# Retention's output projections of two heads by seven half-size products

## The chip, the core and the metric

One core of a Trainium2 chip runs two transformer blocks of two layers each over 512 tokens of width 1024. The metric is device microseconds of one execution; lower is better. All inputs and weights lie in the chip's main memory as 32-bit floats.

## The reference, cut to what matters

The change lies in the retention layer of the second block: four heads, each with 256 query and key features and 512 value features.

```
proj = h @ w_in                              # q, k: 4 x 256; v, g: 4 x 512 columns
q, k = rotate(q), rotate(k) * dk ** -0.5
...                                          # y = decayed attention of each head: scores, decay, values
mu, var = mean(y), var(y)                    # per head
y = ((y - mu) * rsqrt(var + EPS)).reshape(B, S, H * dv)
return (silu(g) * y) @ w_out                 # w_out: 2048 x 1024
```

The last line is what is changed. For head h it is a product of 512 tokens by 512 features (silu(g)*y of that head) with rows 512h to 512h+511 of `w_out`; the four heads' products are added to the residual.

## The kernel before

**Numbers.** Every 32-bit operand is split into two values of a reduced format, hi = round(x) and lo = x - hi, and each product is made of three matmuls, hi·hi, hi·lo and lo·hi. A matmul takes a 128x128 stationary operand and 512 moving columns.

**The weight units.** Weights come in units of up to 128x2048, numbered in one list made by `plan()`; even units use slot 0 and odd units slot 1 of `w_raw`, `w_hi` and `w_lo`. A unit goes through four queues, each of which takes the units in the order of the list:

- SyncE (SP) issues the load into `w_raw` when the unit two places earlier has its low part (semaphore `w_lo_ready`), since then its raw slot is free.
- ScalarE (ACT), in `act_split`, copies `w_raw` to `w_hi` when the load has landed and TensorE has finished the unit two places earlier (`blocks_done`).
- GpSimd (POOL) makes `w_lo = w_raw - w_hi` in four quarters of 512 columns (`split_low`, L749), each of which counts up `w_lo_ready`.
- TensorE (PE) waits in `pe_weights` until the unit's quarters are there.

**Retention.** The head loop is written out as five steps. Step n projects head n and, before and between that, attends with head n-1: scores, query projection `q` (one unit), values, key projection `k`, transposition of the gated values, value projection (units `v0`, `v1`), gate projection (`g0`, `g1`). Steps 1 and 2 end with `output()` for heads 0 and 1: units `o0` and `o1` are the left and right 512 columns of the head's `w_out` rows, each 512 features deep. `output()` runs over 2 halves, 4 token tiles and 4 feature chunks with 3 matmuls each, so 96 matmuls per head (L853 to L855), into PSUM banks 4 to 7; VectorE (DVE) adds each finished bank to the residual (L2528). Heads 2 and 3 are projected in the later steps, which the change leaves as they are.

**Around the place.** The gate projection leaves its four tiles in banks 0, 1, 6 and 7, and ACT takes each through Silu (L2376, semaphore `ret_g_in`). `output()` begins in banks 4 and 5, and waits for `ret_g_in` only ahead of its tiles in banks 6 and 7. After `output()` TensorE makes the next step's scores (L1781, banks 2 to 4) and then the `q` unit (L842 to L844, banks 0 and 1). DVE multiplies the scores by the decay (L3140), ACT copies the result to its hi part (L2342), DVE makes its lo part (L3143); the values' matmuls (L1795) need them.

Of the kernel before, what the change touches and what calls it, by code (L numbers as in the profile page):

```python
# [138 lines left out]
RET_LAST_BANKS = (6, 7, 4, 5, 0, 1, 2, 3)  # L139
RA_PARTS = ((0, 512), (512, 512), (1024, 256))  # L140
# [99 lines left out]
def plan():  # L240
# [70 lines left out]
    for h in range(RH + 1):  # L311
        if h < RH:
            for x in "qk":
                unit(f"ret.{x}{h}"), done(f"ret.{x}{h}", 0, 1)
            for x in "vg":
                for part in range(2):
                    unit(f"ret.{x}{part}{h}"), done(f"ret.{x}{part}{h}", *range(TT))
        if h:
            for half in range(2):
                unit(f"ret.o{half}{h - 1}")  # L320
                if h < RH:
# [15 lines left out]
for _n, (_name, _dmas) in enumerate(UNITS):  # L337
# [21 lines left out]
           for kind, stages, events in SHARED for n, stage in enumerate(stages) for event, total in events.items()}  # L359

# [30 lines left out]
def memory(nc, ctx, dram):  # L391
# [52 lines left out]
    m.ry, m.rg, m.ra = view(2048, 2048, TT), view(4096, 2048, TT), view(6144, 1280)  # L444
    m.rv_hi, m.rv_lo = (r[:, :].rearrange("p (t d) -> p t d", t=TT) for r in (m.r_hi, m.r_lo))
# [292 lines left out]
def pool_program(m, pool):  # L738
# [80 lines left out]
    plain(last_down(f"sw0.d{G2 - 1}"), INDEX["sw1.d0"])  # L819
# [909 lines left out]
def pe_retention(m, pe, beside):  # L1729
# [4 lines left out]
    def step(i, hs, project, attend, write=True):  # L1734
# [8 lines left out]
        def features(x, j):  # L1743
            names = [f"ret.{x}{n}" for n in hs]
            if j == 0:
                pe_weights(m, pe, names, i)
            if x == "k" and not first:
                left("q_in", 2, j + 1)
            elif not first:
                left_before("g_in", TT, TT)  # L1750
            bank = b[2 + j] if first and x == "k" else b[j]
            pe_features(m, bank[:, :], weight(m, names, 2048, KC), j * P, h, KC)

        def tokens(x, part):
# [3 lines left out]
            for t in range(TT):  # L1758
# [4 lines left out]
                elif part == 0 and hs[0] > 1:  # L1763
                    pe.wait_ge(*m.upto("ret_acc", along(i, [KC * (n - 2) + KC for n in hs])))
# [8 lines left out]
        def scores():  # L1773

            left_before("k_roped", 1, 1)
            for kb in (0, 1, 3, 2):
                bank, at = TURN_AT[kb]
                if kb == 2 and project and hs[0] > 1:
                    pe.wait_ge(*m.upto("ret_acc", along(i, [KC * (n - 2) + 5 for n in hs])))
# [5 lines left out]
        def values():  # L1785
# [3 lines left out]
            for q in range(TT):  # L1789
                if q == 3 and project and hs[0] > 1:  # L1790
                    pe.wait_ge(*m.upto("ret_acc", along(i, [KC * (n - 2) + 6 for n in hs])))
# [27 lines left out]

        def held(half, tiles):  # L1820
# [4 lines left out]
            for n in tiles:  # L1825
                if half:
                    pe.wait_ge(*m.upto("ret_acc", KC * h + n + 1))
# [5 lines left out]
        def last_output():  # L1833
            h = RH - 1
            for n, (half, tile) in enumerate(RET_TAIL):
# [3 lines left out]
                if n < 2:  # L1839
                    pe.wait_ge(*m.upto("ret_acc", KC * (h - 1) + 7 + n))  # L1840
# [43 lines left out]
def pe_program(m, pe):  # L1884
# [24 lines left out]
    pe_input(m, pe, "sw1", "sw1_normed", normed, "ret_acc", KC * RH, "sw1.g0", True)  # L1909
# [419 lines left out]
def act_retention(m, act):  # L2329
    s, b, run = m.sem, m.bank, m.nc.scalar.activation  # L2330

    def step(i, hs, project, attend, write=True):
# [27 lines left out]
        if attend:  # L2360
            for c in range(4):
# [3 lines left out]
                run(m.act_hi[:, c if project else RET_SLOTS[c], :], b[2 + c][:, :], ACT.Copy).then_inc(s("ret_o_hi"), 1)  # L2365
        if project:
            for x in "vg":
                for part in range(2):
                    names = [f"ret.{x}{part}{n}" for n in hs]
                    if (x, part) != ("v", 0):  # L2370
                        split(after(names))
                if x == "g" and attend:
# [39 lines left out]
def act_program(m, act):  # L2412
# [21 lines left out]
    act_rms(m, act, "sw1", "ret_acc", [KC * (RH - 1) + n for n in RET_COMPLETE], "sw1.g0", "sw1.u0")  # L2434
# [666 lines left out]
def dve_retention(m, dve, end):  # L3101
    s, b, v = m.sem, m.bank, m.nc.vector

    def step(i, hs, project, attend, write=True):
# [40 lines left out]
        def held(n):  # L3145
            h = RH - 2
            dve_add_block(m, dve, "ret", n, b[RET_BANKS[n % 4]], [f"ret.o{n // 4}{h}"], n % 4, None, [h], False)

        def low(c, at):
            left_before("o_hi", 4, c + 1)  # L3150
            v.tensor_tensor(m.act_lo[:, at, :], b[2 + c][:, :], m.act_hi[:, at, :].bitcast(F32), ALU.subtract).then_inc(s("ret_o_lo"), 1)
# [5 lines left out]
        else:  # L3157
            held(0), held(1)
# [20 lines left out]
        if project:  # L3179
            take("k")  # L3180
            if attend:
                for c in range(4):
                    low(c, c)
# [4 lines left out]
            if attend and write:  # L3188
                for n in range(KC):
                    dve_add_block(m, dve, "ret", n, b[4 + n % 4], [f"ret.o{n // 4}{h - 1}" for h in hs], n % 4, i, [h - 1 for h in hs], hs[0] == 1)  # L3190
# [9 lines left out]
        def add(n):  # L3200
            half, tile = RET_TAIL[n]
            block = TT * half + tile
            dve_add_block(m, dve, "ret", block, b[RET_LAST_BANKS[n]], [f"ret.o{half}{RH - 1}"], tile, None, None, False, False, KC * (RH - 2) + block + 1)
# [138 lines left out]
```

## Time and profile before

| | before |
|---|---|
| device time, median of 3 runs | 2459.97 us (2458.8 to 2460.01) |
| span of the profiled execution, first to last instruction | 2456.9 us |
| what lies around the span (median minus span) | 3.07 us |
| TensorE busy | 2442.6 us, 99% of the span |
| DVE, ACT, POOL busy | 61%, 40%, 50% |
| mean granted TensorE clock | 0.999 of full speed |

The profiled execution shows a span and no device time of its own beside it; the last 3.07 us of the median are taken as what lies around every span. Busy times of TensorE count overlapping matmuls once; the pace of the matmuls is read from the distance of their starts.

### The profile page before, as it was taken

Reading aid. Unit: us, or ns where it says so; the run is one execution under the profiler, and the core shown is the slowest. Engines: PE = TensorE matmul, PEld = TensorE weight load, DVE = VectorE, ACT = ScalarE, POOL = GpSimd, SP = SyncE. Lnnn points to the kernel's source line nnn. Section 1 sums busy time; section 2 is a strip of 40 time slices with the busy share of each in tenths; the row PEclk is TensorE's granted clock in tenths of the full one; section 3 lists DMA queues with packets and bytes.
Section 4 is the critical chain, followed back from the end, with each engine's and each line's share of the span. In section 5 each row is a group of like instructions: output and inputs, shape, how many; then the busy total and the mean of one; then the engine's idle time right before and its main releaser. Section 6 shows DMA issues by size and latency. Waiting matters only on the chain.

```text
span 2456.9 us, 32036 instructions
## 1 busy us (share of the span) xinstructions
PE 2442.6 (99%) x11945; PEld 2032.3 (83%) x11945; DVE 1490.0 (61%) x1999; ACT 988.5 (40%) x1352; POOL 1232.8 (50%) x879
## 2 busy tenths in 40 slices
PE   9999999999999999999999999999999999999998
PEld 8778888888888888888888888888888888888887
DVE  6657777786585777784334566666224133466667
ACT  4445444444565444444324333333332223433332
POOL 4224555644333555553323566665444443566664
PEclk9999999999999999999999999999999999999999
DMA  5212333332222233333221322333222322233222
GB/s 182 68 52 91 103 102 102 103 120 87 70 69 86 86 103 102 102 103 104 69 69 60 126 96 96 102 103 122 93 86 69 103 69 86 95 103 101 96 97 83
DMA packets 173704, 230.94 MB, mean 94 GB/s; under 512 B 11670, under 2 KB 128540, under 8 KB 173468
## 3 DMA queue, kind: packets, MB, share of 16 engines
q1 hardware_dynamic: 173596, 229.44, 28.5%
q8 instruction: 75, 1.23, 0.2%
q14 instruction: 33, 0.27, 0.0%
HBM read 227.32 MB, written 2.10 MB: 93 GB/s over the span
## 4 chain that ended last, share of the span: by engine, by line
PE 65%; issue 20%; POOL 11%; DVE 2%; ACT 0%; DMA 0%; POOLq 0%; SPq 0%; DVEq 0%; ACTq 0%
PE banks L842 11%; PE banks L843 11%; PE banks L844 11%; POOL w_lo L749 11%; PE banks L1640 6%; PE banks L1639 6%; PE banks L1641 6%; PE banks L853 1%; PE banks L855 1%; PE banks L854 1%; PE banks L1125 1%; PE banks L1146 1%; PE banks L1094 1%; PE banks L1081 1%; PE banks L1100 1%
## 5 line engine op out<-in xcount | busy, mean ns | idle before, releaser
L749 POOL TENSOR_TENSOR w_lo<-w_raw,w_hi 128x512 fp32r<-128x512 f32 (+1 forms) x820 | 1163.9, 1451 | 1204.8 <-ACT w_hi L1921 1187.6
L1921 ACT ACTIVATE w_hi<-w_raw 128x2048 fp32r<-128x2048 f32 x204 | 390.4, 1914 | 457.5 <-PE banks L844 176.7
L842 PE MATMUL banks<-h_hi,w_hi 128*128 128x512 f32 x1448 | 567.3, 392 | 0.3 <-POOL w_lo L749 0.3
L844 PE MATMUL banks<-h_hi,w_lo 128*128 128x512 f32 x1448 | 563.5, 389 | 0.0
L843 PE MATMUL banks<-h_lo,w_hi 128*128 128x512 f32 x1448 | 563.4, 389 | 0.0
L842 PEld LDWEIGHTS banks<-h_hi,w_hi 128*128 128x128 f32 x1448 | 271.8, 188 | 62.0 <-issue 4.2
L843 PEld LDWEIGHTS banks<-h_lo,w_hi 128*128 128x128 f32 x1448 | 271.9, 188 | 56.9 <-issue 1.2
L844 PEld LDWEIGHTS banks<-h_hi,w_lo 128*128 128x128 f32 x1448 | 271.8, 188 | 56.8
L2528 DVE TENSOR_TENSOR x_residual<-x_residual,banks 128x512 f32<-128x512 f32 x103 | 69.9, 685 | 132.1 <-PE banks L855 85.7
L3026 DVE TENSOR_TENSOR work<-banks,work 128x512 f32<-128x512 f32 x44 | 30.4, 691 | 191.7 <-PE banks L844 191.7
L1639 PE MATMUL banks<-w_hi,act_hi 128*128 128x512 f32 x352 | 136.9, 389 | 0.0
L1640 PE MATMUL banks<-w_lo,act_hi 128*128 128x512 f32 x352 | 136.9, 389 | 0.0
L1641 PE MATMUL banks<-w_hi,act_lo 128*128 128x512 f32 x352 | 136.9, 389 | 0.0
L3068 DVE TENSOR_TENSOR work<-work,banks 128x1024 f32<-128x1024 f32 x80 | 97.7, 1221 | 18.7 <-PE banks L1641 9.9
L2225 ACT ACTIVATE act_hi<-work 128x1280 fp32r<-128x1280 f32 x26 | 33.2, 1276 | 184.1 <-DVE work L2935 184.1
L1639 PE MATMUL banks<-split_hi,act_hi 128*128 128x512 f32 x264 | 102.7, 389 | 0.0
L1640 PE MATMUL banks<-split_lo,act_hi 128*128 128x512 f32 x264 | 102.7, 389 | 0.0
L1641 PE MATMUL banks<-split_hi,act_lo 128*128 128x512 f32 x264 | 102.7, 389 | 0.0
L2629 DVE CUSTOM_DVE_ANT_0 work<-banks,consts 128x128 f32<-128x128 f32 (+3 forms) x128 | 57.4, 488 | 70.9 <-PE banks L1136 25.7
L1768 PE MATMUL banks<-w_hi,h_hi 128*128 128x512 f32 x256 | 99.9, 390 | 0.0
L1770 PE MATMUL banks<-w_hi,h_lo 128*128 128x512 f32 x256 | 99.6, 389 | 0.0
L1769 PE MATMUL banks<-w_lo,h_hi 128*128 128x512 f32 x256 | 99.6, 389 | 0.0
(330 smaller groups left out, 4672.1 us busy)
## 6 DMA issues: line engine op xcount, KB each, us to landing
w_raw<-in_ffn_w_in SPq DMA_DIRECT2D x44, 1024.0 KB, 5.1
w_raw<-in_ffn_w_up SPq DMA_DIRECT2D x32, 1024.0 KB, 5.3
w_raw<-in_ffn_w_down SPq DMA_DIRECT2D x52, 512.0 KB, 4.4
w_raw<-in_ret_w_in SPq DMA_DIRECT2D x24, 1024.0 KB, 5.1
w_raw<-in_ffn_w_out SPq DMA_DIRECT2D x36, 512.0 KB, 4.4
w_raw<-in_diff_w_qkv SPq DMA_DIRECT2D x12, 1024.0 KB, 5.1
w_raw<-in_fox_w_in SPq DMA_DIRECT2D x12, 1024.0 KB, 5.3
w_raw<-in_ret_w_out SPq DMA_DIRECT2D x8, 1024.0 KB, 5.0
```

The lines of the kernel that those rows point to most:

```text
L749: nc.gpsimd.tensor_tensor(m.w_lo[:, sl, at], m.w_raw[:, sl, at], m.w_hi[:, sl, at].bitcast(F32), ALU.subtract)\
L842: mm(out, hi, x[0][:, k, :], start=k == 0, stop=False)
L843: mm(out, hi, x[1][:, k, :], start=False, stop=False)
L844: last = mm(out, lo, x[0][:, k, :], start=False, stop=k == kc - 1)
L1639: mm(out, hi, w[0], start=begin, stop=False)
L1640: mm(out, hi, w[1], start=False, stop=False)
L1641: last = mm(out, lo, w[0], start=False, stop=end)
L1768: mm(out, hi, w[0][:, k, :], start=part == 0 and k == 0, stop=False)
L1769: mm(out, hi, w[1][:, k, :], start=False, stop=False)
L1770: last = mm(out, lo, w[0][:, k, :], start=False, stop=part == 1 and k == 3)
L1921: m.nc.scalar.activation(m.w_hi[:, sl, 0:width], m.w_raw[:, sl, 0:width], ACT.Copy).then_inc(m.sem("w_hi_ready"), 1)
L3068: v.tensor_tensor(out, out, bank, ALU.add).then_inc(s(f"{t}_evicted"), 1)
```

## The change

For heads 0 and 1 the product is split in halves in tokens, features and columns. With X11, X12, X21, X22 the quarters of the head's features (first index: tokens 0 to 255 or 256 to 511; second: features) and W11 to W22 those of its weights, seven products of half size take the place of eight:

| product | left factor | right factor | unit, part | banks |
|---|---|---|---|---|
| P1 | X11 | W11 | o0, 0 | 2, 3 |
| P2 | X12 | W21 | o0, 1 | 4, 5 |
| P5 | S1 = X21 + X22 | T1 = W12 - W11 | o1, 0 | 6, 7 |
| P3 | S4 = X12 - S2 | W22 | o1, 1 | 0, 1 |
| P6 | S2 = S1 - X11 | T2 = T3 + W11 | c, 0 | 2, 3 |
| P4 | X22 | T4 = W21 - T2 | c, 1 | 4, 5 |
| P7 | S3 = X11 - X21 | T3 = W22 - W12 | d, 0 | 6, 7 |

Each product is 2 token tiles of 2 feature chunks with 3 matmuls: 12 matmuls, 84 per head. Two units per head are new, `c` (128x2048, made by DVE in the raw slot of `o0`) and `d` (128x1024, T3 in a token buffer); they have no load. DVE makes S1 to S4 and T1 to T4, and adds the products in 11 operations instead of 8.

```diff
@@ plan()
+            if h <= RET_PRODUCED:
+                unit(f"ret.c{h - 1}", 0), unit(f"ret.d{h - 1}", 0)
+                for x, part in OUT_ORDER:
+                    done(f"ret.{x}{h - 1}", part)
@@ pool_program
+        for part in range(QUARTERS):
+            at = slice(256 * part, 256 * part + 256)
+            nc.gpsimd.tensor_tensor(m.w_lo[:, d % 2, at], m.out_t3[:, at], m.w_hi[:, d % 2, at].bitcast(F32), ALU.subtract)\
+                .then_inc(s("w_lo_ready"), 1)
@@ pe_retention, scores()
+            if project and hs[0] > 1:
+                pe.wait_ge(*m.upto("ret_added", NADDS * (hs[0] - 2) + out_added(OUT_P4)))
@@ pe_retention, output()
             left_before("o_lo", 4, 4)
-            for half in range(2):
-                names = [f"ret.o{half}{n - 1}" for n in hs]
-                pe_weights(m, pe, names, i)
-                for n in range(4):
-                    if half:
-                        left_before("acc", KC, n + 1)
-                    elif n >= 2:
-                        left("g_in", TT, n + 1)
-                    pe_tokens(m, b[4 + n][:, :], weight(m, names, 2048, 4), (m.act_hi[:, 0:4, :], m.act_lo[:, 0:4, :]), 4, n, 512)\
-                        .then_inc(s("blocks_done"), 1)
+            left_before("o_summed", 5, 5)
+            left("g_in", TT, TT)
+            for product in OUT_ORDER:
+                unit, part = product
+                name, bank, x = f"ret.{unit}{head}", OUT_BANKS[product], x_of[product]
+                pe_weights(m, pe, [name], None, QUARTERS if part or unit == "d" else 2)
...
+                held_by = {OUT_P6: OUT_P1, OUT_P4: OUT_P2, OUT_P7: OUT_P5}.get(product)
+                if held_by:
+                    pe.wait_ge(*m.upto("ret_added", NADDS * head + out_added(held_by)))
+                for t in range(2):
+                    last = pe_tokens(m, b[bank + t][:, :], w, x, 2, t, 512)
+                last.then_inc(s("blocks_done"), 1)
@@ act_retention
-            split(after([f"ret.o0{n - 1}" for n in hs]))
+            head = hs[0] - 1
             if write:
-                split(after([f"ret.o1{n - 1}" for n in hs]))
+                act.wait_ge(*m.upto("ret_o_mixed", 4 * head + 2))
+            split([f"ret.o1{head}"])
+            if write:
+                act.wait_ge(*m.upto("ret_o_mixed", 4 * head + 4))
+                split([f"ret.c{head}"])
+                act.wait_ge(*m.upto("blocks_done", BLOCK[f"ret.o1{head}", 0]))
+                run(m.w_hi[:, slot([f"ret.d{head}"]), 0:1024], m.out_t3, ACT.Copy).then_inc(s("w_hi_ready"), 1)
+                split(after([f"ret.d{head}"]))
@@ dve_retention
+            if project and hs[0] > 1:
+                dve.wait_ge(*m.upto("ret_added", NADDS * (hs[0] - 1)))
...
             if attend and write:
-                for n in range(KC):
-                    dve_add_block(m, dve, "ret", n, b[4 + n % 4], ...
+                feature_sums(), feature_sums_low()
+                out_weight_sums(hs[0] - 1)
+                add_products(hs[0] - 1)
```

On TensorE, at the start of step 1's `output()` (the last matmul of `g1`, then the first of `o0`; `w_hi`, `act_hi` are the stationary and moving parts), the rows of before are:

```order
L1770 MATMUL banks<-w_hi,h_lo 128x512
L853 MATMUL banks<-w_hi,act_hi 128x512 [waits w_lo_ready,ret_o_lo]
L854 MATMUL banks<-w_lo,act_hi 128x512
L855 MATMUL banks<-w_hi,act_lo 128x512
L853 MATMUL banks<-w_hi,act_hi 128x512
```

and of the changed kernel:

```order
L1809 MATMUL banks<-w_hi,h_lo 128x512
L890 MATMUL banks<-w_hi,act_hi 128x512 [waits ret_g_in,w_lo_ready,relu_mlp_mixed,ret_o_lo]
L891 MATMUL banks<-w_lo,act_hi 128x512
L892 MATMUL banks<-w_hi,act_lo 128x512
L890 MATMUL banks<-w_hi,act_hi 128x512
```

The wait for `ret_g_in` (all four Silu tiles) has moved from the 25th matmul of the stage to its first. `relu_mlp_mixed` is a semaphore that the sums S1 to S4 share with an earlier stage.

On ACT, from the last Silu of step 1 to the first operation of step 2 (`work<-banks` is Silu, each `w_hi<-w_raw` a unit's high part), before, where the three units are `o1`, the next step's `q` and its `k`:

```order
L2376 ACTIVATE work<-banks 128x512 [waits blocks_done] x3
L1921 ACTIVATE w_hi<-w_raw 128x2048 [waits blocks_done,w_landed1]
L1921 ACTIVATE w_hi<-w_raw 128x2048 [waits blocks_done,w_landed0]
L1921 ACTIVATE w_hi<-w_raw 128x2048 [waits blocks_done,w_landed1]
L2342 ACTIVATE act_hi<-work 128x512 [waits ret_decayed] x2
```

and of the changed kernel, where they are `o1`, `c`, `d`, `q` and `k`:

```order
L2433 ACTIVATE work<-banks 128x512 [waits blocks_done] x3
L1972 ACTIVATE w_hi<-w_raw 128x2048 [waits blocks_done,w_landed1,relu_mlp_w_mixed]
L1972 ACTIVATE w_hi<-w_raw 128x2048 [waits blocks_done,w_landed0,relu_mlp_w_mixed]
L2444 ACTIVATE w_hi<-tokbuf 128x1024 [waits blocks_done]
L1972 ACTIVATE w_hi<-w_raw 128x2048 [waits blocks_done,w_landed0]
L1972 ACTIVATE w_hi<-w_raw 128x2048 [waits blocks_done,w_landed1]
L2393 ACTIVATE act_hi<-work 128x512 [waits ret_decayed] x2
```

`q` now stands behind `c` and `d`. Its slot (slot 0) was that of `o0` and is now that of `c`, so its load, its high part and its low part each wait for `c` where they waited for `o0`.

## Rows read from the trace of the kernel before

**Rows 1.** The page: span, and busy time of TensorE.

```profile
span 2456.9 us, 32036 instructions
PE 2442.6 (99%) x11945; PEld 2032.3 (83%) x11945; DVE 1490.0 (61%) x1999; ACT 988.5 (40%) x1352; POOL 1232.8 (50%) x879
```

**Rows 2.** The page: the chain that ended last, by engine.

```profile
PE 65%; issue 20%; POOL 11%; DVE 2%; ACT 0%; DMA 0%; POOLq 0%; SPq 0%; DVEq 0%; ACTq 0%
```

**Rows 3.** TensorE's waits, the longest in total: us, times, longest one.

```profile
PE banks L878 <- DVE x_residual L2575: 2.6, 6, 1.0
```

**Rows 4.** Busy time by stretch: step 1's output, step 2's scores, step 2's output.

```profile
core 0: us, PE busy (x) PEld busy (x) DVE busy (x) ACT busy (x) POOL busy (x), PEclk, DMA share, GB/s
...
1841.36:1863.12 21.76, 21.76 (x98) 18.02 (x96) 4.82 (x7) 4.32 (x3) 10.07 (x8) 1.00 0.30 97
1863.12:1867.24 4.12, 4.12 (x17) 2.55 (x16) 1.85 (x3) 2.54 (x2) 1.88 (x2) 1.00 0.25 97
1941.30:1963.10 21.80, 21.80 (x97) 18.05 (x97) 4.81 (x7) 4.32 (x3) 10.07 (x8) 1.00 0.31 97
```

**Rows 5.** TensorE in order of time: start, us; gate's last matmul, output's first.

```profile
1841.13 0.39 PE L1770 MATMUL banks<-w_hi,h_lo 128*128 128x512 f32 x1
1841.36 0.39 PE L853 MATMUL banks<-w_hi,act_hi 128*128 128x512 f32 x1
```

**Rows 6.** ACT in order of time: the last Silu, then units o1 and q.

```profile
1841.56 0.60 ACT L2376 ACTIVATE work<-banks 128x512 f32<-128x512 f32 x1 [2.12 <-PE banks L1770]
1842.05 1.91 ACT L1921 ACTIVATE w_hi<-w_raw 128x2048 fp32r<-128x2048 f32 x1
1852.50 1.92 ACT L1921 ACTIVATE w_hi<-w_raw 128x2048 fp32r<-128x2048 f32 x1 [8.54 <-PE banks L855]
```

**Rows 7.** A wait's end on TensorE elsewhere: the releasing DVE operation, then the matmul.

```profile
202.95 1.29 DVE L2575 SCALAR_TENSOR_TENSOR x_residual<-work,x_columns,tokbuf 128x1024 f32<-128x1024 f32 x1
...
204.38 0.30 PE L878 MATMUL banks<-consts,x_residual 128*128 128x128 f32 x1 [1.03 <-DVE x_residual L2575]
```

**Rows 8.** POOL in order of time: four quarters each.

```profile
1464.34 7.03 POOL L749 TENSOR_TENSOR w_lo<-w_raw,w_hi 128x512 fp32r<-128x512 f32 x4 [3.07 <-ACT w_hi L1921]
...
1765.82 5.92 POOL L749 TENSOR_TENSOR w_lo<-w_raw,w_hi 128x512 fp32r<-128x512 f32 x4 [6.28 <-ACT w_hi L1921]
...
1854.49 5.03 POOL L749 TENSOR_TENSOR w_lo<-w_raw,w_hi 128x512 fp32r<-128x512 f32 x4 [5.41 <-ACT w_hi L1921]
1865.36 5.46 POOL L749 TENSOR_TENSOR w_lo<-w_raw,w_hi 128x512 fp32r<-128x512 f32 x4 [5.85 <-ACT w_hi L1921]
```

**Rows 9.** SP: the issue of one load (v0 of step 2).

```profile
1859.69 0.37 SPq L521 DMA_DIRECT2D w_raw<-in_ret_w_in  x1
```

**Rows 10.** Loads, median us from issue to landing: 1800 to 1950 us, then 1837 to 1848 us.

```profile
w_raw<-in_ret_w_in SPq DMA_DIRECT2D x9, 1024.0 KB, 5.2
w_raw<-in_ret_w_out SPq DMA_DIRECT2D x4, 1024.0 KB, 5.0
...
w_raw<-in_ret_w_in SPq DMA_DIRECT2D x1, 1024.0 KB, 6.3
```

**Rows 11.** DVE in order of time around step 1's output.

```profile
1820.43 0.69 DVE L3186 TENSOR_TENSOR split_lo<-banks,split_hi 128x512 fp32r<-128x512 f32 x1 [2.03 <-ACT split_hi L2376]
1844.28 0.69 DVE L2528 TENSOR_TENSOR x_residual<-x_residual,banks 128x512 f32<-128x512 f32 x1 [23.16 <-PE banks L855]
...
1865.03 0.69 DVE L3140 TENSOR_TENSOR work<-banks,tokbuf 128x512 f32<-128x512 f32 x1 [1.03 <-PE banks L1781]
...
1867.97 3.74 DVE L3143 TENSOR_TENSOR act_lo<-work,act_hi 128x512 fp32r<-128x512 f32 x3
```

**Rows 12.** Groups of DVE by shape: count, busy us, mean ns, idle before.

```profile
L3068 DVE TENSOR_TENSOR work<-work,banks 128x1024 f32<-128x1024 f32 x80 | 97.7, 1221 | 18.7 <-PE banks L1641 9.9
...
L2907 DVE TENSOR_TENSOR tokbuf<-w_raw 128x1024 f32<-128x1024 f32 x44 | 73.2, 1663 | 0.0
...
L3077 DVE TENSOR_TENSOR x_residual<-x_residual,work 128x1024 f32<-128x1024 f32 x20 | 38.5, 1978 | 0.0
```

More of the change, by code:

```diff
@@ L2371, in step @@
                         split(after(names))
+                    if (x, part) == ("g", 0) and attend and write:
+                        left_before("o_summed", 5, 5)
+                        run(m.act_hi[:, 4:7, :], m.ry[:, 0:3, :], ACT.Copy).then_inc(s("ret_o_sums_hi"), 1)
+                        run(m.act_hi[:, 0:2, 256:512], m.ry[:, 3, :].rearrange("p (k t) -> p k t", k=2), ACT.Copy)\
+                            .then_inc(s("ret_o_sums_hi"), 1)
                 if x == "g" and attend:
@@ new lines, in feature_sums @@
+        def feature_sums():
+            done = s("ret_o_summed")
+            a11, a21, a12, a22 = (m.banks[:, c:c + 2, at:at + 256] for c, at in ((2, 0), (2, 256), (4, 0), (4, 256)))
+            s1, s2, s3, s4 = (m.ry[:, n, :].rearrange("p (k t) -> p k t", k=2) for n in range(4))
+            left_before("turned", 4, 4)
+            v.tensor_copy(s4, a21).then_inc(done, 1)
+            left_before("o_summed", 5, 1)
+            v.tensor_tensor(s1, s4, a22, ALU.add).then_inc(done, 1)
+            v.tensor_tensor(s3, a11, s4, ALU.subtract).then_inc(done, 1)
+            left_before("o_summed", 5, 2)
+            v.tensor_tensor(s2, s1, a11, ALU.subtract).then_inc(done, 1)
+            left_before("o_summed", 5, 4)
+            v.tensor_tensor(s4, a12, s2, ALU.subtract).then_inc(done, 1)
@@ new lines, in feature_sums_low, with out_weight_sums @@
+        def feature_sums_low():
+            left_before("o_sums_hi", 2, 1)
+            v.tensor_tensor(m.act_lo[:, 4:7, :], m.ry[:, 0:3, :], m.act_hi[:, 4:7, :].bitcast(F32), ALU.subtract).then_inc(s("ret_o_sums_lo"), 1)
+            left_before("o_sums_hi", 2, 2)
+            v.tensor_tensor(m.act_lo[:, 0:2, 256:512], m.ry[:, 3, :].rearrange("p (k t) -> p k t", k=2),
+                            m.act_hi[:, 0:2, 256:512].bitcast(F32), ALU.subtract).then_inc(s("ret_o_sums_lo"), 1)
+        def out_weight_sums(head):
+            names, done = [f"ret.o{half}{head}" for half in range(2)], s("ret_o_mixed")
+            for name in names:
+                dve.wait_ge(*m.upto(f"w_landed{slot([name])}", LANDED[INDEX[name]]))
+            (b11, b21), (b12, b22) = [[m.w_raw[:, slot([name]), at:at + 1024] for at in (0, 1024)] for name in names]
+            dve.wait_ge(*m.upto("ret_k_roped", head + 2))
+            v.tensor_tensor(m.out_t3, b22, b12, ALU.subtract).then_inc(done, 1)
+            left_before("o_mixed", 4, 1)
+            v.tensor_tensor(b12, b12, b11, ALU.subtract).then_inc(done, 1)
+            left_before("o_mixed", 4, 2)
+            dve.wait_ge(*m.upto("w_lo_ready", QUARTERS * (INDEX[names[0]] + 1)))
+            v.tensor_tensor(b11, m.out_t3, b11, ALU.add).then_inc(done, 1)
+            left_before("o_mixed", 4, 3)
+            v.tensor_tensor(b21, b21, b11, ALU.subtract).then_inc(done, 1)
@@ new lines, in add_products @@
+        def add_products(head):
+            kept = m.out_p1
+            if head:
+                dve.wait_ge(*m.upto("ret_added", NADDS * head))
+            for n, (source, into) in enumerate(OUT_ADDS):
+                if source == "kept":
+                    more = kept
+                else:
+                    unit, part = source
+                    dve.wait_ge(*m.upto("blocks_done", BLOCK[f"ret.{unit}{head}", part]))
+                    more = m.banks[:, OUT_BANKS[source]:OUT_BANKS[source] + 2, :]
+                earlier = [k + 1 for k in range(n) if out_touched(k) & out_touched(n) - {source if source != "kept" else None}]
+                if earlier:
+                    dve.wait_ge(*m.upto("ret_added", NADDS * head + max(earlier)))
+                if into == "last rows":
+                    x, more = m.x[:, 2:4, :].rearrange("p t (a n) -> p t a n", a=2), kept.unsqueeze(2).broadcast_to([P, 2, 2, 512])
+                else:
+                    x = kept if into == "kept" else quadrant(m, into)
+                if n:
+                    v.tensor_tensor(x, x, more, ALU.add).then_inc(s("ret_added"), 1)
+                else:
+                    v.tensor_copy(x, more).then_inc(s("ret_added"), 1)
@@ L3157, in step @@
         else:
+            dve.wait_ge(*m.upto("ret_added", NADDS * RET_PRODUCED))
             held(0), held(1)
@@ L3182, in step @@
                 for c in range(4):
-                    low(c, c)
+                    low(c, c, 256 if write and c < 2 else T)
             for tile in range(TT):
```

65 lines of the change are left out of this document (48 added, 17 removed).

## Prediction

> **What bounds the kernel now.** The page comes first: TensorE is busy for 2442.6 of 2456.9 us [rows 1], so 14.3 us of the whole span are its idle time. The chain that ended last runs 65% over TensorE and 11% over GpSimd's low parts [rows 2]; the latter are weights that came just in time. The list of TensorE's waits says whether they hold it up: the largest sum is 2.6 us over six waits, the longest one is 1.0 us, and no line of retention stands there [rows 3]. So a matmul that goes shortens the kernel by its pace, and a new wait of TensorE lengthens it by nearly all of its length.
>
> Then the stage itself, by stretches [rows 4]. Step 1's 96 output matmuls take 21.76 us, TensorE busy throughout, at granted clock 1.00 (2.4 GHz): 0.2267 us each. Step 2's differ by 0.04 us, so one head is worked out and doubled. The scores behind them take 4.12 us. DVE is busy for 4.82, ACT for 4.32, POOL for 10.07 of the 21.76 us, so there is room for added work; what matters is its order and its latency.
>
> **What is removed.** 12 matmuls per head, 12 x 0.2267 = 2.72 us, 5.44 us for both. That is 0.22% of the time, and about 0.2% is what a measurement of this kernel can tell from no change; the whole gain would barely show.
>
> **A wait that is moved.** All four Silu tiles must now be out before the first matmul. The last gate matmul starts at 1841.13 and the first of the output followed at 1841.36 [rows 5]. The last Silu starts at 1841.56 and takes 0.60 [rows 6], so it ends at 1842.16. A matmul that waited for DVE started 0.14 us behind the end of its releaser (202.95 + 1.29 = 204.24, then 204.38) [rows 7]. So the first product starts at 1842.30, 0.94 us later than before. All of TensorE's queue stands behind it, and nothing covers it. Bounds: 0.80 without the restart, 0.94 with it.
>
> **The path of the weights.** From 1842.30 a product takes 2.72 us: P1 and P2 end at 1847.74, P5 at 1850.46, P3 at 1853.18, P6 at 1855.90, P4 at 1858.62, P7 at 1861.34; the scores end at 1865.46. Then TensorE wants the next step's `q`. Before, its chain began when `o0` was done: ACT made its high part at 1852.50 [rows 6], POOL was through at 1854.49 + 5.03 = 1859.52 [rows 8], 7.7 us ahead of the use at 1867.24. Now it begins with `c`, in the same slot:
>
> - ACT may split `c` when P2 is done. The o0 unit's last matmul starts at 1841.36 + 47 x 0.2267 = 1852.01 and ACT started at 1852.50, so 0.49 after that start, 0.26 after the pace's end: 1848.00.
> - POOL starts 1.99 us after ACT (1852.50 to 1854.49) and takes 5.03: `c` is ready at 1855.02. P6 wants two quarters, there at 1852.51, at 1853.18, and P4 all of them at 1855.90, so both are covered, by 0.7 and 0.9 us.
> - SP may load `q` only then, 0.17 us later (1859.52 to 1859.69 [rows 9]), at 1855.19. The load takes 5.2 us [rows 10]: 1860.39. P4, which must also be done, ends earlier.
> - ACT, then POOL after 1.99 us: 1860.44 to 1862.43. POOL's pass next to the decays took 5.46 [rows 8], so `q` is ready at 1867.89, and TensorE goes on at about 1867.95.
>
> TensorE stands from 1865.46 to 1867.95: **a new wait of 2.5 us**. Bounds: with a load of 5.0 us [rows 10] and 5.03 for POOL it is 1.8; with 6.3 us for the load, seen once for this very `q`, and 5.92 for both of POOL's passes [rows 8], it is 4.9. I take the middle rows, since they are of the same operations in the same place.
>
> Behind `q` on SP stands the load of `k`, which waits for `d`; it and its two splits follow `q` by some 5.5 us, so `k` is ready near 1873.4 and is wanted 48 x 0.2267 = 10.9 us after `q` starts, at 1878.8. No wait there.
>
> **POOL's neighbour.** The pass at 1854.49 ran while DVE added output tiles, each with one input in PSUM, and took 5.03; that at 1765.82, during DVE's low parts with both inputs in SBUF, took 5.92 [rows 8]. While `c` is in POOL, DVE adds products out of PSUM, so I take 5.03 for it.
> The Trainium skill (GPSIMD Engine Reference, Specifications) states the rule: the SBUF interface is shared, and a DVE instruction with two SBUF inputs contends. The trace agrees, with those 5.03 and 5.92. By the rule the pass over `q` could reach 5.92 as well, since the last add has both inputs in SBUF; the sum below would then be 0.9 us larger over both heads.
>
> **Covered edits.** S1 to S4, their splits and T1 to T4 fall into the gate projection, where DVE was idle for 23.16 us up to 1844.28 [rows 11]. From 1821.1: five 512-wide operations at 0.69, low parts of about 2.5 together, then four 1024-wide at up to 1.66 [rows 12]; T1 to T4 start when `o1` has landed, at about 1832.6, T2 waits for POOL's pass over `o0`, and T4 is done near 1841, 7 us before ACT wants `c`. `o1` splits behind the last Silu as before (1842.05 [rows 6]); its first two quarters are there at 1846.6, P5 wants them at 1847.74. Without these covers each us would be a us of TensorE. `d`'s four 256-wide quarters have no row: between half of a 512-wide quarter (2.5 us for four) and a full one (5.0), in POOL from 1855.02. At worst P7 is late by 1.5 us, and the wait for `q`, which doesn't depend on P7, shortens by as much: nothing either way. I take the lower, nearer by size.
>
> The adds are nine at 1.22, one of 1024 from SBUF (up to 1.98) and one of twice that [rows 12]. Banks are freed in time: the P4 add that the scores wait for ends at about 1860.3, they start at 1861.34. The last adds end near 1866; behind them on DVE stand the decays, which began at 1865.03, and ACT's copies. The low parts they lead to ended at 1867.97 + 3.74 = 1871.7 [rows 11]; 2 us later is still ahead of the values' matmuls at 1878.8.
>
> **The sum.** Per head -2.72 + 0.94 + 2.49 = +0.71 us, +1.4 us for both, on a span of 2456.9: 2458.3. With the 3.07 us that lie around the span the median is 2461.4 us. By the bounds a head comes to between -0.1 and +3.1.
>
> **Rivals.**
> - *Only the Silu wait is new.* `q` would have to be ready 2.5 us sooner than the rows say, sooner even than the lower bound by 1.8. For it: each link was read with other neighbours. Then 2 x (-2.72 + 0.94) = -3.6: 2456.4 us. Chance 0.08.
> - *Neither wait*: -5.4, 2454.5 us. The order of semaphores speaks against it, since the Silu tile can't be out before its matmuls end. Chance 0.04.
> - *Slower: POOL held up by DVE on the way to `q`.* The worst pass in the rows took 7.03 us [rows 8], next to two-input sums. If both the `c` and the `q` pass took that, it would be 2.0 and 1.6 us more per head, +8.6 in all: 2468.6 us. It decides from 1.75 us per head on, where the total passes +4.9. Against: DVE's adds at `c` read PSUM. Chance 0.13.
> - *Slower: the clock falls in the new waits.* TensorE now stands twice in 24 us, once for 2.5 us. If one `q` unit's 48 matmuls then ran at 1.2 GHz, each head would pay 48 x 0.2267 = 10.9 us: 2483 us. Eight matmuls per head at that level (1.8 us) already decide. Against: the granted clock is 1.00 in every stretch [rows 4]. But the longest wait so far is 1.0 us [rows 3]. Chance 0.04. The Trainium skill (TensorE: Matmul & The Clock Gate, Part 1) says that idleness brings the lower level; no stretch here shows it.
>
> **The numbers.** My forecast, two new waits that eat the gain, has 0.71, and its own range by its bounds is 2459.8 to 2466.2. The range reaches down to the first rival and leaves out the most extreme end above, where every link would be at its worst: 2456.4 to 2465.4. Faster by over 0.2% (below 2455.0): the second rival and a little, 0.05. Slower (above 2464.9): the last two and the forecast's upper tail, 0.18. Within: 0.77.
>
> **What the profile after would show.** TensorE waiting for ACT's Silu tile ahead of the first product, 0.9 us, twice. Ahead of L879, the first matmul of `q`, a wait for POOL of 2 to 3 us, twice. 84 matmuls per output at the old pace, with no wait of over 0.3 us between products. SP issuing `q` some 17 us later against the stage's start than before. DVE idle up to the sums, with T4 done before the first product. The prediction is wrong if TensorE waits inside the products (then `c` or `d` is late, or a bank), if it waits at the values (the adds delay the decays), or if the clock in that stretch is below 1.00.

## The result, and the profile after

| | before | after |
|---|---|---|
| device time, median of 4 runs each | 2459.39 us (2458.2 to 2460.01) | 2470.89 us (2468.18 to 2472.17) |
| ratio, 95% interval | | 1.0045 [1.0033, 1.0057] |
| span of the profiled execution | 2456.9 us | 2466.4 us |
| mean granted TensorE clock | 0.999 | 0.998 |

The changed kernel is slower by 0.45%, 9.5 us above the forecast and above its range. Of these 9.5 us, 8.1 lie in the span (2466.4 where 2458.3 was worked out). The other 1.4 are the distance from span to median. Each of the four executions of after took 1.8 us more than its own span, and the profiled one, at 2468.18, was the shortest of them; the longest had a mean clock of 0.996. The medians lie 11.5 us apart and the profiled spans 9.5; what follows explains those 9.5, and no trace shows the other executions of after.

The page of after, its span and busy times:

```profile
span 2466.4 us, 32058 instructions
...
PE 2441.4 (99%) x11921; PEld 2030.1 (82%) x11921; DVE 1535.1 (62%) x2027; ACT 997.3 (40%) x1360; POOL 1259.2 (51%) x895
```

TensorE has lost its 24 matmuls, yet its busy time fell by only 1.2 us against [rows 1], not by 5.4: some of the matmuls that are left ran more slowly. And 25.0 us of the span are idle now, where 14.3 were. Its waits in the two stages (1835 to 1990 us), total, times, longest:

```profile
PE banks L879 <- POOL w_lo L776: 9.3, 2, 5.0
PE banks L890 <- ACT work L2433: 1.8, 2, 0.9
```

There are two waits per head and no others, at the two places that were forecast: the first product behind Silu (0.9 us) and `q` behind POOL. The second is twice as long as forecast, and TensorE runs more slowly behind it. Windows of after (columns as in [rows 4]): the products of both heads, then the wait of head 0 and what follows it.

```profile
1842.35:1861.40 19.05, 19.05 (x84) 15.81 (x85) 11.09 (x9) 5.21 (x4) 12.90 (x12) 1.00 0.26 85
1946.55:1965.60 19.05, 19.02 (x84) 15.80 (x85) 11.09 (x9) 4.56 (x3) 12.90 (x12) 1.00 0.25 84
1865.90:1870.20 4.30, 0.06 (x1) 0.00 (x0) 4.27 (x7) 1.57 (x3) 4.30 (x4) 0.94 0.00 0
1870.20:1872.90 2.70, 2.70 (x6) 2.16 (x7) 1.92 (x2) 0.00 (x0) 2.70 (x2) 0.50 0.52 116
```

The 84 matmuls take 19.05 us where 96 took 21.76 [rows 4]. After the wait the granted clock is 0.50, the level of 1.2 GHz, and six matmuls fill the 2.70 us in which twelve have room. In head 1 eight start at that pace. TensorE in order of time, the first matmuls of `q` in head 0, then the first of head 1:

```profile
1870.20 0.80 PE L879 MATMUL banks<-h_hi,w_hi 128*128 128x512 f32 x1 [4.25 <-POOL w_lo L776]
1870.80 0.63 PE L880 MATMUL banks<-h_lo,w_hi 128*128 128x512 f32 x1
1871.22 0.63 PE L881 MATMUL banks<-h_hi,w_lo 128*128 128x512 f32 x1
...
1975.23 0.62 PE L879 MATMUL banks<-h_hi,w_hi 128*128 128x512 f32 x1 [5.04 <-POOL w_lo L776]
```

Why `q` was late is read off POOL and DVE. POOL's quarters of `q`, the first two of head 0 and the first of head 1:

```profile
1862.71 1.27 POOL L776 TENSOR_TENSOR w_lo<-w_raw,w_hi 128x512 fp32r<-128x512 f32 x1 [4.71 <-ACT w_hi L1972]
1863.94 3.32 POOL L776 TENSOR_TENSOR w_lo<-w_raw,w_hi 128x512 fp32r<-128x512 f32 x1
...
1968.48 2.11 POOL L776 TENSOR_TENSOR w_lo<-w_raw,w_hi 128x512 fp32r<-128x512 f32 x1 [6.24 <-ACT w_hi L1972]
```

DVE's last add (the sum kept for `"last rows"`, both inputs in SBUF), in head 0 and in head 1:

```profile
1862.94 3.19 DVE L3278 TENSOR_TENSOR x_residual<-x_residual,work 128x2048 f32<-128x2048 f32 x1
...
1967.17 2.29 DVE L3278 TENSOR_TENSOR x_residual<-x_residual,work 128x2048 f32<-128x2048 f32 x1
```

A quarter that meets nothing takes 1.27 us. That of 1863.94 took 3.32 and ended at 1867.26, 1.13 after the add (1862.94 + 3.19 = 1866.13); that of 1968.48 ended at 1970.59, again 1.13 after the add (1967.17 + 2.29 = 1969.46). So a quarter that meets the add does its work when the add is over. The add of head 0 in turn began while the quarter of 1862.71 ran, and took 0.9 us more than that of head 1, which found POOL idle.

**A ledger for one head.** To compare kernels, one stretch serves: from the start of the last Silu on ACT to DVE's first use of `q` (line L3124 before, L3188 after). In what follows it is called *the stage*. DVE's row at its end, first of before, head 0:

```profile
1873.19 0.69 DVE L3124 SCALAR_TENSOR_TENSOR tokbuf<-banks,tokbuf 128x512 f32<-128x512 f32 x1 [1.48 <-PE banks L844]
```

and of after, heads 0 and 1:

```profile
1877.36 0.69 DVE L3188 SCALAR_TENSOR_TENSOR tokbuf<-banks,tokbuf 128x512 f32<-128x512 f32 x1 [5.24 <-PE banks L881]
...
1982.70 0.69 DVE L3188 SCALAR_TENSOR_TENSOR tokbuf<-banks,tokbuf 128x512 f32<-128x512 f32 x1 [7.24 <-PE banks L881]
```

With the last Silu at 1841.56 before [rows 6] and 1841.50 after, head 0's stage went from 31.63 to 35.86 us. Head 1's went from 31.64 to 36.97, its Silu being at 1945.73. That is +4.23 and +5.33, together 9.56 where the span grew by 9.5: on balance nothing was lost elsewhere.

### The profile page after: what moved, and what is told of

Read it like the earlier page. It is cut to its first block, busy times and chain, and to the rows that moved or that the text cites. A ratio compares the mean times of both kernels' runs of the same rounds, so it can differ in the third digit from the quotient of the medians.

```text
span 2466.4 us, 32058 instructions
## 1 busy us (share of the span) xinstructions
PE 2441.4 (99%) x11921; PEld 2030.1 (82%) x11921; DVE 1535.1 (62%) x2027; ACT 997.3 (40%) x1360; POOL 1259.2 (51%) x895
## 4 chain that ended last, share of the span: by engine, by line
PE 76%; issue 14%; POOL 7%; DVE 2%; ACT 0%; DMA 0%; POOLq 0%; SPq 0%; DVEq 0%; ACTq 0%
PE banks L879 12%; PE banks L880 12%; PE banks L881 12%; POOL w_lo L776 7%; PE banks L1677 6%; PE banks L1678 6%; PE banks L1676 6%; PE banks L890 2%; PE banks L1809 2%; PE banks L1807 2%; PE banks L892 2%; PE banks L1808 2%; PE banks L891 2%; PE banks L1162 1%; PE banks L929 1%
## 5 line engine op out<-in xcount | busy, mean ns | idle before, releaser
L776 POOL TENSOR_TENSOR w_lo<-w_raw,w_hi 128x512 fp32r<-128x512 f32 (+1 forms) x828 | 1184.8, 1463 | 1187.9 <-ACT w_hi L1972 1170.6
L879 PE MATMUL banks<-h_hi,w_hi 128*128 128x512 f32 x1448 | 568.3, 392 | 9.6 <-POOL w_lo L776 9.6
L879 PEld LDWEIGHTS banks<-h_hi,w_hi 128*128 128x128 f32 x1448 | 272.7, 188 | 72.3 <-POOL w_lo L776 11.3
L3014 DVE TENSOR_TENSOR split_lo<-tokbuf,split_hi 128x1536 fp32r<-128x1536 f32 x26 | 46.9, 1802 | 85.1 <-ACT split_hi L2284 85.1
```

The costliest lines, as they stand in the source:

```text
L776: nc.gpsimd.tensor_tensor(m.w_lo[:, sl, at], m.w_raw[:, sl, at], m.w_hi[:, sl, at].bitcast(F32), ALU.subtract)\
L879: mm(out, hi, x[0][:, k, :], start=k == 0, stop=False)
```

## The experiments

The theory after this reading: three separate costs, each of which can be taken away alone, namely the wait for Silu, the late `q` (its load hangs on `c`, and its low part meets DVE's last add), and the lower clock behind that wait. The rivals: that a cost which is taken away only uncovers the next one, that POOL's pass or the load is not what ends the wait, and that the clock falls for another reason than the standstill. All experiments are edits of the changed kernel. Ratios are to the kernel before, timed beside them (median 2459.73 us for e1 to e4, 2458.8 for e5 to e7). Spans compare less well than stages do: the last Silu of head 0 starts anywhere from 1841.0 to 1843.6 us in these executions. It starts at 1842.5 or later in the profiles of e2, e3, e4 and e5, and in these the granted clock also falls near 1144 us (0.50 from 1144 to 1146 in e2), far ahead of the changed place; in the other five it is 1.00 there. So spans of e2 to e5 carry 1 to 2 us that are not the edit's.

| kernel | median us | ratio, interval | span | stage, heads 0 and 1 | wait at `q` |
|---|---|---|---|---|---|
| before | 2459.39 | | 2456.9 | 31.63, 31.64 | none |
| after | 2470.89 | 1.0045 [1.0033, 1.0057] | 2466.4 | 35.86, 36.97 | 4.25, 5.04 |
| e1_silu | 2467.6 | 1.0033 [1.0021, 1.0046] | 2465.4 | 36.28, 35.65 | 4.24, 5.02 |
| e2_early | 2463.97 | 1.0018 [1.0008, 1.0027] | 2462.7 | 34.11, 34.03 | 2.13, 2.13 |
| e3_psum | 2464.29 | 1.0016 [1.0007, 1.0026] | 2463.2 | 32.03, 35.56 | 1.68, 3.61 |
| e4_busy | 2465.73 | 1.0024 [1.0015, 1.0034] | 2464.3 | 34.59, 34.60 | filled |
| e6_early_psum | 2459.97 | 1.0002 [0.9992, 1.0011] | 2457.3 | 31.80, 31.75 | 1.44, 1.44 |
| e5_all | 2457.58 | 0.9992 [0.9983, 1.0002] | 2456.2 | 30.65, 30.67 | 1.43, 1.44 |
| e7_halves | 2453.82 | 0.9981 [0.9971, 0.9990] | 2451.5 | 29.44, 29.45 | none listed |

**e1_silu: the wait for all Silu tiles, moved to the third product.** P1 and P2 write banks 2 to 5, so only P5, in banks 6 and 7, needs it.

```diff
-            left("g_in", TT, TT)
             for product in OUT_ORDER:
...
                 if product == OUT_P5:
+                    left("g_in", TT, TT)
                     left_before("o_sums_lo", 2, 1)
```

> The changed kernel with one edit: the wait for the four Silu tiles stands ahead of P5 (the first product in their banks) instead of ahead of P1. Theory A (the chain that ends at the next step's q starts with P2's end: c's high and low part, then the load of q, its high and low part): the 0.9 us wait before P1 goes and the whole chain moves forward with it, so TensorE's wait at q keeps its length of 4 to 5 us and the span falls by 2 x 0.95 = 1.9 us, from 2466.4 to about 2464.5. Rival B (q's end is set by something that does not follow the products): the wait at q grows by the 0.9 us per head and the span stays within 0.5 us of 2466.4.

TensorE, first matmul of `q` in both heads:

```profile
1868.93 0.79 PE L879 MATMUL banks<-h_hi,w_hi 128*128 128x512 f32 x1 [4.24 <-POOL w_lo L776]
...
1974.34 0.80 PE L879 MATMUL banks<-h_hi,w_hi 128*128 128x512 f32 x1 [5.02 <-POOL w_lo L776]
```

The wait for Silu is gone and the wait at `q` is as long as in after, so the latter doesn't absorb the former: the chain to `q` hangs on the products and moves with them. Counted from the last Silu (1841.33 here), head 0's `q` starts 27.60 us later, against 28.70 in after: 1.10 us, near the 0.95 expected. Even so the span fell by 1.0 us and not by 1.9: in head 0 the stage isn't shorter, and the window behind the wait says why:

```profile
1868.93:1874.90 5.97, 5.97 (x14) 4.71 (x15) 1.92 (x2) 0.00 (x0) 5.52 (x4) 0.50 0.57 178
```

Fourteen matmuls at 1.2 GHz, where after had six behind a wait of the same length. What the clock costs varies, even with the same wait.

**e2_early: `q` and `k` loaded before the products.** `c` gets a buffer of its own (free token storage), so the raw slots are free when the low parts of `o0` and `o1` and the sums are done. A loop on SP is written out, so that the new waits can be placed, and ACT and POOL read `c` from its new place; these parts of the edit are left out here.

```diff
@@ SP's loads
+        early = names[0][:5] in ("ret.q", "ret.k") and int(names[0][5:]) > 1
+        if early:
+            head = int(names[0][5:]) - 2
+            sp.wait_ge(*m.upto("w_lo_ready", QUARTERS * (INDEX[f"ret.o{int(names[0][4] == 'k')}{head}"] + 1)))
+            sp.wait_ge(*m.upto("ret_o_mixed", 4 * head + 4))
+        elif INDEX[names[0]] >= 2:
@@ DVE's sums of weights (T2, T4)
-            v.tensor_tensor(b11, m.out_t3, b11, ALU.add).then_inc(done, 1)
+            left_before("o_sums_lo", 2, 2)
+            v.tensor_tensor(m.out_c[:, 0:1024], m.out_t3, b11, ALU.add).then_inc(done, 1)
...
-            v.tensor_tensor(b21, b21, b11, ALU.subtract).then_inc(done, 1)
+            v.tensor_tensor(m.out_c[:, 1024:2048], b21, m.out_c[:, 0:1024], ALU.subtract).then_inc(done, 1)
```

> The changed kernel with T2 and T4 written to a buffer that is free by then instead of o0's raw slot, and q and k loaded as soon as o0 and o1 have their low parts and the sums are made (SyncE's loop of three heads written out for it). Theory A (the load behind c is the late link): q is loaded near 1843 us instead of 1855.5, its high part starts when P4 is done, near 1859, 1.8 us sooner in the first head and 3.8 us in the second, and the wait at q falls from 4.3 and 5.0 us to 2 to 3 us; with less of the 1.2 GHz clock behind it the span falls by 5 to 8 us, to 2458 to 2461. Rival C (only GpSimd's stretched pass over q is late, the load is covered): the waits stay at 4 us or more and the span falls by less than 2 us.

SP issues the load of `q` at 1843.34, 12.2 us earlier than in after (1855.51). TensorE's first matmul of `q` in both heads:

```profile
1869.10 0.50 PE L890 MATMUL banks<-h_hi,w_hi 128*128 128x512 f32 x1 [2.13 <-POOL w_lo L782]
...
1971.58 0.50 PE L890 MATMUL banks<-h_hi,w_hi 128*128 128x512 f32 x1 [2.13 <-POOL w_lo L782]
```

The wait is halved, and both heads are now alike. So the load was on the path, and the difference between the heads came from it: in after it took 5.2 us in head 0 and 6.7 in head 1. What is left is ACT's and POOL's part: ACT may write `q` into the slot of `c` only when P4 is done, and one quarter of `q` still takes 3.3 us in each head. Behind a wait of 2.13 us the clock still falls, in both heads, and more than 1 us after TensorE has started again:

```profile
1870.80:1873.50 2.70, 2.70 (x8) 2.12 (x7) 1.91 (x2) 0.00 (x0) 2.70 (x2) 0.50 0.94 350
1972.80:1975.50 2.70, 2.70 (x8) 2.05 (x8) 2.39 (x2) 0.00 (x0) 2.70 (x3) 0.50 0.95 317
```

The span fell by 3.7 us, less than the 5 to 8 expected: the low clock costs as much as before, and the Silu comes 1.0 us later than in after. The two stages together are 4.69 us shorter.

**e3_psum: the add with two SBUF inputs out of `q`'s way.** The kept sum goes to `"last rows"` before P7 instead of behind it, and P7 is added twice, straight from PSUM: 12 adds in place of 11.

```diff
-            (OUT_P6, "kept"), ("kept", (0, 1)), (OUT_P4, (1, 0)), (OUT_P7, "kept"), ("kept", "last rows"))
+            (OUT_P6, "kept"), ("kept", (0, 1)), (OUT_P4, (1, 0)), ("kept", "last rows"), (OUT_P7, (1, 0)), (OUT_P7, (1, 1)))
```

> The changed kernel with its last add re-ordered: the kept sum goes to the last token rows before P7 is done (while GpSimd has nothing to do), and P7 is then added out of PSUM to both quarters, 12 adds instead of 11. Theory C (the 2048-wide DVE add with both inputs in SBUF holds GpSimd's second quarter of q, 3.3 us instead of 1.26): that quarter falls to 1.3 us, the pass over q to 5.0 to 5.6 us, TensorE's wait at q by some 2 us in the first head and 1 to 2 in the second, the span by 3 to 4 us to about 2463. Rival: the pass is slow for another reason and q's quarters still add up to 6.5 us or more; the span stays within 1 us.

The first two quarters of `q` in head 0, then DVE in the same stretch:

```profile
1864.70 1.27 POOL L776 TENSOR_TENSOR w_lo<-w_raw,w_hi 128x512 fp32r<-128x512 f32 x1 [4.62 <-ACT w_hi L1972]
1865.93 1.28 POOL L776 TENSOR_TENSOR w_lo<-w_raw,w_hi 128x512 fp32r<-128x512 f32 x1
```

```profile
1862.32 2.29 DVE L3278 TENSOR_TENSOR x_residual<-x_residual,work 128x2048 f32<-128x2048 f32 x1
1864.72 2.35 DVE L3278 TENSOR_TENSOR x_residual<-x_residual,banks 128x1024 f32<-128x1024 f32 x2
```

With POOL idle the add takes 2.29 us, and beside the two adds out of PSUM (1864.72 to 1867.07) the quarters take their 1.27: the source of the add, not DVE's being busy, held POOL up. Head 0 is almost back at before's stage (32.03), with a wait of 1.68 us behind which the clock stays at 1.00. In head 1 the load took 6.6 us, the wait was 3.61 us, and the clock fell:

```profile
1869.70:1872.40 2.70, 2.68 (x12) 2.18 (x13) 2.70 (x3) 0.00 (x0) 2.70 (x2) 1.00 0.49 115
1972.05:1974.75 2.70, 2.70 (x9) 2.19 (x10) 1.92 (x2) 0.00 (x0) 2.70 (x2) 0.75 0.49 121
```

**e4_busy: the wait filled with matmuls.** Twenty matmuls of 512 columns whose result nobody reads go into bank 5 ahead of each wait for `q`; nothing else is changed.

```diff
+                if x == "q" and attend and hs[0] > 1:
+                    for _ in range(20):
+                        mm(b[5][:, :], m.h_hi[:, 0, 0:P], m.h_hi[:, 0, :], start=True, stop=True)
                 pe_weights(m, pe, names, i)
```

> The changed kernel with 20 idle matmuls of 512 columns (4.5 us) into a free bank ahead of each wait for q of steps 2 and 3; they compute nothing that is used. Theory D (the long stand lets the clock fall to 1.2 GHz, and the first 6 to 8 matmuls of q then start 0.43 instead of 0.23 us apart): the granted clock stays at 1.00, the first matmuls of q start 0.23 us apart and the span falls by 1.2 + 1.6 = 2.8 us to about 2463.6, although the time at which q's weights are ready does not move. Rival: the slow start comes with the wait itself (weights or queue), and the span stays within 0.5 us.

The stretch that was the wait, and the one behind it:

```profile
1867.50:1871.90 4.40, 4.40 (x21) 3.52 (x20) 4.37 (x7) 1.57 (x3) 4.40 (x4) 1.00 0.00 0
1871.90:1874.60 2.70, 2.70 (x13) 2.27 (x13) 1.83 (x2) 0.00 (x0) 2.70 (x2) 1.00 0.54 140
```

`q` comes no sooner, but the clock holds at 1.00 and the matmuls of `q` follow at 0.22 to 0.23 us from the first one on. From the first matmul of `q` to DVE's use of it head 0 takes 5.70 us where after took 7.16, head 1 5.71 where after took 7.47. So at this place it is the standstill that lowers the clock. Head 0's stage is 1.27 us shorter than in after, head 1's 2.37, since its load took 5.1 us this time and `q` started 0.6 us sooner after the Silu. The span fell by 2.1 us where 2.8 were expected, with the Silu 1.55 us later than in after. The medians differ by 5.2 us, more than the 3.64 of the stages; after's profiled execution was its shortest, and no trace shows where the others lost more.

**e6_early_psum: e2 and e3 together.**

> Both edits to the path of q at once: the early load of e2_early and the re-ordered last add of e3_psum; the Silu wait stays ahead of P1. If load and held GpSimd pass are the two causes of the long wait, q is ready 0.26 + 1.99 + 5.05 = 7.3 us after P4 and wanted 6.85 us after it: a wait of 0.4 to 1.0 us, short enough that the clock stays at 1.00. Per head -2.72 + 1.05 + 0.6 = -1.1 us against before: span about 2454.8, the median some 2 us below before, 2457.5. If the products themselves, the adds or something not yet seen cost time, the span stays above 2457.

The wait at `q` is 1.44 us in both heads, longer than the 0.4 to 1.0 expected; no clock falls behind it. The stage is 31.80 and 31.75: the two new waits just use up the 2.72 us of matmuls, and the kernel is where it was before. Most of the wait is the add again. The early load lets POOL start on `q` sooner, at 1861.25, and there it meets the add in its new place:

```profile
1860.45 2.29 DVE L3291 TENSOR_TENSOR x_residual<-x_residual,work 128x2048 f32<-128x2048 f32 x1
```

```profile
1861.25 2.63 POOL L782 TENSOR_TENSOR w_lo<-w_raw,w_hi 128x512 fp32r<-128x512 f32 x1 [3.05 <-ACT w_hi L1983]
```

The first quarter takes 2.63 us, 1.36 too many, and ends 1.14 us after the add. So e3's edit moves the collision out of the way only as long as `q` is late.

**e5_all: e6 with e1's edit.**

> e6_early_psum with the Silu wait moved ahead of P5 too. Now that q's end hangs on P4, the 0.95 us per head of the Silu wait should come back in full: span about 2453, median about 2455.7. If the Silu wait was hidden behind the wait at q, it gives nothing over e6_early_psum.

The stage falls by another 1.15 and 1.08 us (30.65, 30.67), which gives the Silu wait its own size once no clock blurs it. The median fell short of the 2455.7 us expected, and the interval of the ratio still includes 1. Of the 2.72 us per head 1.74 are missing, and that is the wait at `q`: 1.43 us listed, and some 0.35 by which `q` overlapped the scores before. Head 0's first quarter took 2.63 us beside the add, as in e6.

**e7_halves: e5, with the high part of `q` in halves.** ACT writes the first half when P6 no longer reads `c`'s first half, the second after P4, and POOL follows by halves. The wait for the load and POOL's subtraction are left out of the edit shown.

```diff
@@ ACT, in place of split(q)
...
+                for half, sem in enumerate(("ret_q_half", "w_hi_ready")):
+                    act.wait_ge(*m.upto("blocks_done", BLOCK[f"ret.c{head}", half]))
+                    at = slice(1024 * half, 1024 * half + 1024)
+                    run(m.w_hi[:, slot([q]), at], m.w_raw[:, slot([q]), at], ACT.Copy).then_inc(s(sem), 1)
@@ POOL
+        pool.wait_ge(*m.upto("ret_q_half", head + 1))
+        for part in range(QUARTERS):
+            if part == 2:
+                pool.wait_ge(*m.upto("w_hi_ready", d + 1))
...
```

> e5_all, and q's high part made in two halves, the first as soon as P6 is done (GpSimd follows by halves too). The rest of the wait at q, 0.4 to 1.0 us per head, goes: no wait of TensorE in the stage is left, all 24 removed matmuls count, 2 x 2.72 = 5.4 us: span about 2451.5, median about 2454, a ratio of 0.998 to before. If it stays over 2453 in span, part of the 5.4 us goes somewhere that is not a wait at q or at P1.

TensorE over head 0's products and scores, and the first matmul of `q` behind them, ahead of which no idle time is listed:

```profile
1840.83:1864.40 23.57, 23.55 (x101) 18.29 (x99) 17.65 (x13) 9.42 (x7) 20.89 (x17) 1.00 0.27 89
```

```profile
1864.41 0.50 PE L897 MATMUL banks<-h_hi,w_hi 128*128 128x512 f32 x1
```

The stage is 2.19 us shorter than before's in each head, of 2.72 that twelve matmuls are worth, and span and median come out as expected. Most of the last half microsecond is still POOL: its pass over `q`, 1856.31 to 1864.35, met two adds with both inputs in SBUF, took 8.04 us and ended 0.06 before that first matmul, which comes 4.51 us after the first score where it came 4.12 after it before. At 2453.82 us this version beats both kernels (0.9981 of the time before, and its interval excludes 1).

## Why the prediction was wrong, by its own steps

| term, per head | forecast | head 0 | head 1 |
|---|---|---|---|
| twelve matmuls less | -2.72 | -2.63 | -2.63 |
| wait for Silu | +0.94 | +1.05 | +1.05 |
| wait at `q` | +2.49 | +4.60 | +5.39 |
| lower clock behind it | 0 | +1.21 | +1.52 |
| sum | +0.71 | +4.23 | +5.33 |
| the stage, measured | | +4.23 | +5.33 |

Each measured term is a stretch of after less the same stretch of before. The matmuls' stretch runs from the first product to the first score (19.13 us, before 21.76). That of the Silu wait runs from the last Silu to the first product (+0.85 us, before -0.20). That of the wait at `q` runs from the first score to the first matmul of `q` (8.72 and 9.52 us, before 4.12 and 4.13), and that of the clock from there to DVE's use of `q` (7.16 and 7.47 us, before 5.95). The scores of after, in head 0 and head 1:

```profile
1861.48 4.48 PE L1820 MATMUL banks<-work 128*128 128x512 f32 x16
...
1965.71 4.48 PE L1820 MATMUL banks<-work 128*128 128x512 f32 x16
```

The term for `q` is 0.35 us larger than the idle time listed (4.25, 5.04), because before `q` started ahead of the modelled end of the last score matmul:

```profile
1866.34 1.25 PE L1781 MATMUL banks<-work 128*128 128x128 f32 x6
1867.24 0.58 PE L842 MATMUL banks<-h_hi,w_hi 128*128 128x512 f32 x1
```

**The step that failed is "The path of the weights", in its last line: POOL's pass over `q`, put at 5.46 us.** In head 0 it took 7.4 us (1862.71 to 1870.1), 1.95 more. The forecast saw the add with two SBUF inputs and priced what its rule gives at 0.9 us for both heads, by the 5.92 of a pass during DVE's low parts, whose pieces are 512 wide. What counts is the length of the one DVE operation that a quarter meets; this one is 2048 wide, and e3 shows that with adds out of PSUM the quarters stay at 1.27. The mechanism had been named, as the rival "POOL held up by DVE", with 0.13; its price of 1.6 us for the `q` pass was near, while the 2.0 us it set for `c` never came (5.05 where 5.03 was taken). The forecast's own upper bound, 2466.2 us, was passed too, since it held 5.92 for POOL's passes and no lower clock.

**In head 1 the term that was off is the load, put at 5.2 us.** It took 6.7, 1.5 more, and by that delay the quarter met only the add's end (2.11 us instead of 3.32); the whole pass took 6.7 us, 1.2 more than forecast. The bound of 6.3 for the load stood in the text. e2, which takes the load off the path, made the heads equal.

**The clock was held too unlikely.** The sum puts it at nothing. The rival "the clock falls in the new waits" had 0.04, on the ground that the granted clock was 1.00 in every stretch read; but before has no wait above 1.0 us [rows 3], as the forecast itself says, and so tells nothing about longer ones. The rival's small form, 6 and 8 matmuls of `q`, is what came: 1.21 and 1.52 us against before's `q`, near the 1.8 from which by its own words it decides. e4 shows that the standstill is the cause. The two rivals came true together in part, and the forecast had priced each alone.

**A smaller term.** The 3.07 us between span and median are not what lies around a span: in every execution listed of after and of the seven edits the time is 1.7 to 1.9 us longer than its own span. The rest of the 3.07 is a difference between executions.

**What was right.** The place and the kind of both waits, 0.9 us at the first product (listed as 0.89) and POOL at L879. 84 matmuls at the old pace, with no wait inside the products: T4 was done at 1842.26, only 0.09 us before the first of them and 1.3 later than forecast, and `d`'s four quarters took 2.85 us, near the lower bound that was taken. In head 0 the chain up to POOL's start on `q` was 0.28 us late in 20. The adds delayed no values: no wait of TensorE stands there. By causes, the wait at `q` is 2.11 us above the forecast in head 0, 1.95 of it POOL's pass, and 2.90 in head 1, 1.5 of it the load and 1.2 the pass; what is left, 0.2 in each, lies in the smaller links of the chain.

**Still open: why the same load of 1 MB takes 5.2 us in one place and 6.7 in the other.** Head 1's took 6.6 to 6.7 in after, e1 and e3 and 5.1 in e4. The DMA rows of after as head 1's load starts (1958 to 1961 us), then as head 0's does (1854 to 1857):

```profile
q8 instruction: 1, 0.02, 3.7%
...
w_raw<-in_ret_w_in SPq DMA_DIRECT2D x1, 1024.0 KB, 6.7
```

```profile
w_raw<-in_ret_w_in SPq DMA_DIRECT2D x1, 1024.0 KB, 5.2
```

A packet of the instruction queue (q8, 0.02 MB) moved beside the slow load and none beside the fast one. Between 1500 and 2060 us of before, after and e1 to e4, each weight load of 6 us or more has such a packet within 3 us of its issue, or stands right behind a load that has one; e4's packet came near 1955 us, ahead of the load. That points to the instruction loads, but no run moved one, so the cause isn't shown.

## What to carry to other kernels

A new unit in a two-slot weight path costs more than its own work: the next unit's load, high part and low part all start behind it, so add up that whole chain against the time of its use, and see whether a buffer of its own or a split by halves takes the chain apart (here, with the Silu wait and the add moved too, the difference between 1.0045 and 0.9981). Where a low part on GpSimd comes just in time, look at which single DVE operation it can meet: one long operation with two SBUF inputs costs its whole remaining length, an add out of PSUM nothing that could be seen. Look again after each edit, since an earlier pass can meet the same operation in its new place (e6). Price a new wait of TensorE of some microseconds above its length, since the matmuls behind it may run at the lower clock; a profile without such waits is no evidence that they won't.

## What the runs showed of the hardware

**GpSimd and a DVE operation with two SBUF inputs exclude each other, one whole operation at a time.** A 512-wide quarter went from 1.27 to 3.32 us when it came behind the start of a 2048-wide DVE add with two SBUF inputs, and ended 1.13 us after the add in both heads; in e6 the quarter at 1861.25 ended 1.14 after it. The add, coming while a quarter ran, went from 2.29 to 3.19. Beside adds with one input in PSUM the four quarters of `c` took 5.05 us, as before with DVE idle (5.02 at 1832.73). The Trainium skill (SBUF — State Buffer, section "SBUF: two separate sides") calls the shared pair of ports "an exclusive lock, not a bandwidth split", held by whichever starts first for its whole instruction. These rows agree with it in both directions.

**The clock after a standstill.** It fell to 1.2 GHz behind waits of 4.24 to 5.04 us (in after for 6 and 8 matmuls, in e1's head 0 for 14), and of 3.61 and 2.13 us, there more than 1 us after TensorE had started again. It stayed at 2.4 GHz behind 1.68 and 1.44 us, and where matmuls filled a wait of over 4 us. Against before's `q`, the cost behind a wait was between nothing and 2.7 us, and its length alone does not set it: 1.6 and 1.5 us behind 2.13, but 1.2 behind 4.25 and 2.7 behind 4.24. The Trainium skill (TensorE: Matmul & The Clock Gate, Part 1) says that an idle TensorE comes back at the lower level and that how many matmuls it then costs differs from run to run; the waits of 2.13 us and more agree with both, those of 1.68 us and less did not lower the clock.

**The clock also fell where no wait is listed.** Near 1141 us TensorE makes seven matmuls of only 8 columns in 2.1 us (in e2 from 1140.31 to 1142.45). Behind them the granted clock was 0.50 for part of the next 5 us in the profiles of e2, e3, e4 and e5 and 1.00 in the other five, though all have the same matmuls there. So a list of waits does not show every place where the clock can fall.
